# Eight smallest experts on 64 slots, with unsplit float32 weights on column parts of TensorE, placed among the dense tiles

## The chip, the cores and the metric

The kernel runs on one core of one Trainium2 chip. The metric is the device time of one execution in microseconds (us). One profiled execution of the kernel before is read besides; its time is given beside its span.

## What is computed

Two blocks follow each other on 256 tokens of width 1024, in float32: a first block (attention, a linear recurrence, a mixture of experts) and a second block of two layers. The change touches the mixture of experts alone. Cut to that, the reference is:

```python
def hierarchical_moe(h, w_group, b_group, w_er, b_er, w_gate, w_up, w_down):
    # one group of 4 experts for a token, and the 2 best experts in it
    ...
    combine_w = jnp.sum(jax.nn.one_hot(expert_id, N_EXPERTS) * top_w[..., None], axis=1)
    def expert_block(args):
        xs, cs = args
        a = jnp.einsum('nd,edf->nef', xs, w_gate)     # 16 experts, 1024 -> 512
        u = jnp.einsum('nd,edf->nef', xs, w_up)
        hid = jax.nn.silu(a) * u * cs[:, :, None]
        return jnp.einsum('nef,efd->nd', hid, w_down) # 512 -> 1024
```

A token has a nonzero weight for two of the 16 experts only. Each expert has 6 MB of weights: gate, up and down.

## The kernel before, in words

**Tiles.** All large weights are read as tiles of 1 MB (512 x 512 float32, laid out as 128 partitions x 4 x 512). SyncE's queue issues their loads in one fixed order into four landing buffers (`weights_raw`, `RAW_SLOTS = 4`), tile i into buffer i % 4 (`load_tile`). The product of two float32 numbers is made of three products of shorter ones: ScalarE rounds each half of a landed tile to `fp32r` (`high`, into `weights_high`), VectorE subtracts it from the landed numbers (`low`, into `weights_low`), and TensorE multiplies high by high, low by high and high by low. A landing buffer is free again when VectorE has made the second low half (`lo_ready`). The split copies lie in rings of two, in the mixture of three (`weights_high_third`).

**The mixture.** `M0 = T_MOE` is its first tile, and it has 96 tiles. The router's counts sort the experts by the number of their tokens. Expert 0 is computed for all 256 tokens before the order is known. Of the sorted list, the three fullest are "dense" (`DENSE = 3`): all 256 tokens, 48 matmuls of 256 columns or 24 of 512 for each tile (`feature_tile`, `down_tile`, `token_rows`). The other twelve are "sparse" (`SPARSE = 12`): an expert gets 128 slots; matmuls with one-hot matrices gather its tokens (`gather_chunk`, two experts at a time, four chunks), and a tile is then 12 matmuls whose stationary operand is the slots and whose moving operand is 512 columns of weights (`item_tile`). The hidden numbers go through SiLU on ScalarE and a product on VectorE, are turned by four transposes (`turn_hidden`), split, and multiplied by the two down tiles (`item_down`). GpSimd scatters each expert's rows into an array in HBM (`pairs`), reads it back at the end (`pair_rows`), and VectorE adds the rows, two for each token (`add_pairs`).

**The order.** It is written out by hand on each engine. The twelve sparse experts come first, each one's down tiles after the next one's gate and up tiles; then the three dense experts follow. Near the end stand the up tiles of dense expert 3, the two down tiles of dense expert 2, and the two of expert 3. While TensorE works on expert 2's down tiles, the hidden numbers of expert 3 are made (`dense_hidden` on VectorE, `dense_high` on ScalarE, and the low part on VectorE). `add_pairs` is called before the last dense expert's tiles are split.

## Time and profile before

| | us |
|---|---|
| median of 3 runs | 1275.63 (1275.31 to 1275.70) |
| the profiled execution | 1276.64 |
| its span | 1274.8 |
| TensorE busy | 1212.1 (95%) |
| VectorE busy | 888.7 (70%) |
| ScalarE busy | 783.6 (61%) |
| weights split on VectorE in all (368 + 64 halves) | 443.8 + 77.0 |
| weights split on ScalarE in all | 383.1 + 67.9 |

The profiled execution's time is its span and 1.8 us around it. In the rows below, busy TensorE time is no measure of its peak: matmuls are pipelined, so that one record of 0.39 us starts 0.23 us after the last. The distance between starts is the cost of one, and the idle time in front of an instruction (in brackets) says what ended last there. The span's times are in us from its start. The sparse experts' gate and up tiles run from 347.6, the dense experts after them, and the last tile of the mixture leads to the first rows of the result at 673.4.

### The profile page before, as it was taken

What the parts mean: (1) busy time and instruction counts of PE and PEld (TensorE: products, weight loads), DVE (VectorE), ACT (ScalarE), POOL (GpSimd) and SP (SyncE); (2) the same over time, 40 slices, a digit from 0 to 9 for tenths busy, and PEclk for the clock granted to TensorE, in tenths of its full rate; (3) what the DMA queues carried; (4) which work ended last, traced back from release to release, by engine and by line L of the source; (5) the groups of instructions that cost most, each with busy time, mean ns of one, the idle gap of its engine ahead of it and who ended that gap; (6) DMA issues with size and microseconds to landing.
All of it is one profiled execution on the core that took longest, in us unless ns stands there. A gap on an engine that the chain in (4) does not pass through costs nothing.

```text
span 1274.8 us, 19255 instructions
## 1 busy us (share of the span) xinstructions
PE 1212.1 (95%) x7779; PEld 1081.4 (85%) x7779; DVE 888.7 (70%) x1204; ACT 783.6 (61%) x1226; POOL 32.1 (3%) x42
## 2 busy tenths in 40 slices
PE   7999898998999999999999999999999998999997
PEld 7987788998888888889997888899987887899995
DVE  5839986667999999885576646465586556455676
ACT  6568666645588888884345557556535557555543
POOL 1000000000000000000000000000010000000000
PEclk9999999999999999999999999999999999999999
DMA  9743543443589999997763454444345543445331
GB/s 364 254 164 99 165 133 100 145 161 124 199 293 321 328 349 344 335 365 279 247 197 127 142 177 132 133 133 159 106 137 183 162 166 105 160 132 166 100 133 50
DMA packets 117754, 241.22 MB, mean 189 GB/s; under 512 B 5202, under 2 KB 7282, under 8 KB 116769
## 3 DMA queue, kind: packets, MB, share of 16 engines
q1 hardware_dynamic: 113088, 228.44, 53.1%
q0 software_dynamic: 3376, 8.93, 1.9%
q10 hardware_dynamic: 1200, 2.61, 0.6%
q8 instruction: 62, 1.02, 0.3%
q14 instruction: 28, 0.22, 0.1%
HBM read 235.38 MB, written 9.44 MB: 192 GB/s over the span
## 4 chain that ended last, share of the span: by engine, by line
PE 77%; DVE 13%; ACT 6%; issue 3%; DMA 1%; SPq 0%; DVEq 0%; ACTq 0%
PE psum L562 26%; PE psum L1256 15%; PE psum L488 12%; DVE weights_low L364 4%; PE psum L501 4%; PE psum L2138 3%; PE psum L1246 3%; PE psum L2182 2%; PE psum L2198 2%; PE psum L1273 2%; PE psum L2172 1%; PE psum L2117 1%; PE psum L535 1%; ACT weights_high L355 1%; ACT arena L868 1%
## 5 line engine op out<-in xcount | busy, mean ns | idle before, releaser
L364 DVE TENSOR_TENSOR weights_low<-weights_raw,weights_high 128x1024 fp32r<-128x1024 f32 (+1 forms) x368 | 443.8, 1230 | 154.8 <-ACT weights_high L355 151.8
L355 ACT ACTIVATE weights_high<-weights_raw 128x1024 fp32r<-128x1024 f32 (+1 forms) x368 | 383.1, 1057 | 202.6 <-PE psum L562 88.3
L562 PE MATMUL psum<-act_high,weights_high 128*128 128x256 f32 x912 | 265.6, 291 | 2.2 <-ACT arena L2218 1.6
L562 PE MATMUL psum<-act_low,weights_high 128*128 128x256 f32 x912 | 258.5, 283 | 0.0
L562 PE MATMUL psum<-act_high,weights_low 128*128 128x256 f32 x912 | 258.5, 283 | 0.0
L562 PEld LDWEIGHTS psum<-act_high,weights_high 128*128 128x128 f32 x912 | 175.2, 192 | 6.2 <-issue 3.4
L562 PEld LDWEIGHTS psum<-act_high,weights_low 128*128 128x128 f32 x912 | 175.4, 192 | 0.5 <-issue 0.5
L562 PEld LDWEIGHTS psum<-act_low,weights_high 128*128 128x128 f32 x912 | 175.1, 192 | 0.0
L488 PE MATMUL psum<-weights_high,act_high 128*128 128x512 f32 (+1 forms) x320 | 127.7, 399 | 7.9 <-DVE weights_low L364 5.0
L488 PE MATMUL psum<-weights_high,act_low 128*128 128x512 f32 (+1 forms) x320 | 124.6, 389 | 0.0
L488 PE MATMUL psum<-weights_low,act_high 128*128 128x512 f32 (+1 forms) x320 | 124.5, 389 | 0.0
L355 ACT ACTIVATE weights_high_third<-weights_raw 128x1024 fp32r<-128x1024 f32 x64 | 67.9, 1063 | 50.2 <-PE psum L1256 23.5
L364 DVE TENSOR_TENSOR weights_low_third<-weights_raw,weights_high_third 128x1024 fp32r<-128x1024 f32 x64 | 77.0, 1222 | 22.1 <-ACT weights_high_third L355 21.2
L488 PEld LDWEIGHTS psum<-weights_high,act_high 128*128 128x128 f32 x320 | 60.1, 188 | 23.8 <-DVE weights_low L364 6.8
L488 PEld LDWEIGHTS psum<-weights_high,act_low 128*128 128x128 f32 x320 | 60.0, 188 | 12.7
L488 PEld LDWEIGHTS psum<-weights_low,act_high 128*128 128x128 f32 x320 | 60.2, 188 | 11.4
L1256 PE MATMUL psum<-weights_high,picked_high 128*128 128x512 f32 x144 | 57.1, 396 | 0.0
L1256 PE MATMUL psum<-weights_low,picked_high 128*128 128x512 f32 x144 | 56.8, 395 | 0.0
L1256 PE MATMUL psum<-weights_high,picked_low 128*128 128x512 f32 x144 | 56.8, 394 | 0.0
L2363 ACT ACTIVATE arena<-psum 128x512 f32<-128x512 f32 (+1 forms) x34 | 20.2, 595 | 55.7 <-PE psum L2172 55.7
L2353 ACT ACTIVATE arena<-arena,tiny 128x128 f32<-128x128 f32 (+2 forms) x80 | 33.0, 418 | 17.9 <-DVE tiny L2587 17.8
L2198 PE MATMUL psum<-mid_high,weights_high 128*128 128x256 f32 x128 | 36.5, 286 | 1.9 <-DVE mid_low L456 1.8
(448 smaller groups left out, 2361.3 us busy)
## 6 DMA issues: line engine op xcount, KB each, us to landing
weights_raw<-in_w_in SPq DMA_DIRECT2D x52, 1024.0 KB, 5.2
weights_raw<-in_w_expert_gate SPq DMA_DIRECT2D x32, 1024.0 KB, 6.6
weights_raw<-in_w_expert_up SPq DMA_DIRECT2D x32, 1024.0 KB, 6.5
weights_raw<-in_w_expert_down SPq DMA_DIRECT2D x32, 1024.0 KB, 5.7
weights_raw<-in_w_merge SPq DMA_DIRECT2D x32, 1024.0 KB, 5.0
weights_raw<-in_w_out SPq DMA_DIRECT2D x12, 1024.0 KB, 5.0
weights_raw<-in_w_branch SPq DMA_DIRECT2D x8, 1024.0 KB, 5.1
weights_raw<-in_w_lru_o SPq DMA_DIRECT2D x4, 1024.0 KB, 5.2
```

Source lines behind the costliest of these rows:

```text
L355: nc.scalar.activation(hi_tile(i)[:, half_at(part, n)], raw_tile(i, n)[:, cols], ACT.Copy)\
L364: dve.tensor_tensor(lo_tile(i)[:, half_at(part, n)], raw_tile(i, n)[:, cols], hi_tile(i)[:, half_at(part, n)].bitcast(f32), ALU.subtract). ...
L488: last = pe.matmul(pair(g)[:, t * 512:t * 512 + n], a[:, 4 * h + k, t * P:(t + 1) * P], b[:, chunk_at(k, n)], start=(h == 0 and k == 0 and ...
L501: return pe.matmul(pair(g)[:, t * 512:t * 512 + n], a[:, c0 + 4 * h + k, t * P:(t + 1) * P], b[:, chunk_at(k, n)], start=(h == 0 and k == ...
L562: last = pe.matmul(pair(g)[:, s * SEQ:(s + 1) * SEQ], b[:, k * 512 + s * P:k * 512 + (s + 1) * P], a[:, 4 * h + k, :], start=(h == 0 and k ...
L1246: last = pe.matmul(pair(g)[:, t * 512:(t + 1) * 512], a[:, c0 + k, t * P:(t + 1) * P], b[:, k * 512:(k + 1) * 512], start=(k == 0 and q == 0),
L1256: last = pe.matmul(out, a[:, k0 + k, cols], b[:, k * 512:(k + 1) * 512], start=(first and k == 0 and q == 0), stop=(final and k == 3 and q ...
L1273: last = pe.matmul(bank(5 + n % 2)[:, f * SEQ:(f + 1) * SEQ], part[:, t, fb * P:(fb + 1) * P], one_hots[q % 2][:, t, :], start=(t == 0 and ...
L2138: last = pe.matmul(at[:, h * SEQ:h * SEQ + n], qTs[0:rows_of(kind), h, t * P:(t + 1) * P], keys_of(kind, t, h), start=True, stop=True)
L2182: last = pe.matmul(bank(7)[:, HD * h:HD * h + HD], pTs[0:keys, (hh * kts + kt) * P:(hh * kts + kt + 1) * P], values_of(kind, kt, h), start ...
L2198: last = pe.matmul(pair(g)[:, s * SEQ:(s + 1) * SEQ], b[:, at:at + P], a[:, 2 * br + kc, :], start=(kc == 0 and q == 0 and s % 2 == 0), st ...
L2353: last = nc.scalar.activation(p[:, h, :], p[:, h, :], ACT.Exp, bias=l_nb[:, h:h + 1], accum_out=l_sum[:, h:h + 1])
```

## The change

Of the twelve sparse experts the first four stay as they are (`MEDIUM = 4`). The eight smallest get 64 slots each and are gathered four at a time. Their weight tiles aren't split: TensorE reads them from the landing buffer as plain float32, with the 64 slots as the stationary operand, in two halves that go to two column parts of the array (`tile_position` 0 and 64) and to the lower and the upper 64 partitions of the result. A landing buffer of such a tile is free when TensorE has used it. The dense tiles are now placed among them: behind each small expert's four gate and up tiles stand two dense tiles (even ones) or one (odd ones), then its own two down tiles. The gather of the small experts makes float32 rows (`picked_plain`) without a low part. `add_pairs` is the last but one thing that VectorE does. There are four landing buffers, as before.

```diff
-DENSE, SPARSE = 3, 12
+DENSE, SPARSE, MEDIUM = 3, 12, 4
...
+        SMALL_AT, at = [], T_MOE + 32
+        for j in range(SPARSE - MEDIUM):
+            SMALL_AT.append(at)
+            at += 6 + 2 - j % 2
+        AMID = [n for j, a in enumerate(SMALL_AT) for n in range(a + 4, a + 6 - j % 2)]
...
         def load_tile(sp, i, r=0, source=None):
-            if i >= RAW_SLOTS:
-                sp.wait_ge(lo_ready, halves_of(i - RAW_SLOTS + 1, r))
+            if i - RAW_SLOTS in PLAIN:
+                sp.wait_ge(tile_used, halves_of(i - RAW_SLOTS + 1))
+            elif i >= RAW_SLOTS:
+                sp.wait_ge(lo_ready, split_halves(i - RAW_SLOTS + 1, r))
...
+        def small_tile(pe, i, out, stationary, first, final):
+            pe.wait_ge(raw_ready[i % RAW_SLOTS], 16 * (i // RAW_SLOTS + 1))
+            for k in range(4):
+                for h in range(2):
+                    at = 512 * k + 256 * h
+                    last = pe.matmul(out[64 * h:64 * h + 64, :], stationary(k), raw_tile(i)[:, at:at + 256],
+                                     start=(first and k == 0), stop=(final and k == 3), tile_position=(0, 64 * h),
+                                     skip_group_check=True)
+            last.then_inc(tile_used, 2)
...
+            for k in range(4):
+                at = P * (k % 2) + 64 * (k // 2)
+                for n, tile in enumerate(tiles_n):
+                    last = pe.matmul(small_out_bank(i)[64 * n:64 * n + 64, :], hidT_n[:, at:at + 64],
+                                     raw_tile(tile)[:, 512 * k:512 * k + 512], start=(k == 0), stop=(k == 3),
+                                     tile_position=(0, 64 * n), skip_group_check=True)
...
             if c == 3:
-                for j in range(2):
-                    for t in range(NT):
-                        last = pe.matmul(bank(7)[:, 64 + 4 * q + 2 * j:66 + 4 * q + 2 * j],
-                                         one_hots[q % 2][:, t, j * P:(j + 1) * P], rows_r[:, t, DENSE + 2 * q + j, :],
-                                         start=(t == 0), stop=(t == 1))
+                for i in members(q):
+                    n = slots_of(i).stop - slots_of(i).start
+                    for at in range(0, P, n):
+                        for t in range(NT):
+                            last = pe.matmul(bank(7)[at:at + n, 64 + 2 * i:66 + 2 * i],
+                                             one_hots[q % 2][:, t, slots_of(i)].bitcast(f32),
+                                             rows_r[:, t, DENSE + i, :].bitcast(f32), start=(t == 0), stop=(t == 1),
+                                             tile_position=(0, at))
...
         def moe_pe(pe):
...
+            for i in range(MEDIUM, SPARSE):
+                beside, *more = AMID_TILES[i - MEDIUM]
+                small_gate_up(pe, i)
+                dense_tile(*beside, 0, 2)
+                turn_small(pe, i)
+                dense_tile(*beside, 2, 4)
+                for tile in more:
+                    dense_tile(*tile)
+                small_down(pe, i)
+            for h in range(2):
+                dense_tile(DENSE, "u", h)
             pe.wait_ge(hid_lo, DENSE + 2)
...
         def moe_act(act):
...
+            for i in range(MEDIUM, SPARSE):
+                beside, *more = AMID_TILES[i - MEDIUM]
+                high(act, DENSE_AT[beside])
+                small_silu(act, i)
+                for tile in more:
+                    high(act, DENSE_AT[tile])
+                if i == SPARSE - 1:
+                    high(act, M0 + 92)
+                small_turned(act, i)
...
+                small_out(act, i)
...
         def moe_dve(dve, own):
...
+            for n in range(93, 96):
+                low(dve, M0 + n)
+            dense_hidden(dve, DENSE)
+            dve.wait_ge(block_free[(DB_DOWN[DENSE - 1] + 1) % 2], (DB_DOWN[DENSE - 1] + 1) // 2 + 1)
+            add_pairs(dve, own)
```

TensorE's row before, in the sparse stage, where an expert's gate tile ends, the last expert's hidden numbers are turned and the next tile begins:

```order
L1256 MATMUL psum<-weights_high,picked_low 128x512
L1348 MATMUL psum<-params,arena 128x128 [waits sparse_hidden_low,sparse_hidden]
L1348 MATMUL psum<-params,arena 128x128 x3
L1256 MATMUL psum<-weights_high_third,picked_high 128x512 [waits lo_ready]
L1256 MATMUL psum<-weights_low_third,picked_high 128x512
```

TensorE's row now, from the last split tile of a sparse expert over the four unsplit gate and up tiles of the first small one to its first dense tile:

```order
L1289 MATMUL psum<-weights_high,mid_low 128x512
L1299 MATMUL psum<-weights_raw,arena 64x256 [waits raw_ready0,picked_high]
L1299 MATMUL psum<-weights_raw,arena 64x256 x7
L1299 MATMUL psum<-weights_raw,arena 64x256 [waits raw_ready1,picked_high]
L1299 MATMUL psum<-weights_raw,arena 64x256 x7
L1299 MATMUL psum<-weights_raw,arena 64x256 [waits raw_ready2]
L1299 MATMUL psum<-weights_raw,arena 64x256 x7
L1299 MATMUL psum<-weights_raw,arena 64x256 [waits raw_ready3]
L1299 MATMUL psum<-weights_raw,arena 64x256 x7
L577 MATMUL psum<-act_high,weights_high_third 128x256 [waits lo_ready,block_free1,sparse_out]
```

TensorE now waits for the landing itself (`raw_ready`) at each unsplit tile, and for a split one (`lo_ready`) right behind them.

ScalarE's row now, at the last small expert: its SiLU, the split of the first up tile of dense expert 3, and only then the copy of the turned hidden numbers (L1592):

```order
L1586 ACTIVATE arena<-psum 128x256 [waits sparse_hidden,tile_used]
L370 ACTIVATE weights_high_third<-weights_raw 128x1024 [waits tile_used,raw_ready0]
L370 ACTIVATE weights_high_third<-weights_raw 128x1024 [waits tile_used]
L1592 ACTIVATE arena<-psum 128x256 [waits tile_used,sparse_turned]
L1535 ACTIVATE arena<-psum 128x1024 [waits hidden_low,tile_used]
L1597 ACTIVATE arena<-psum 128x512 [waits scattered1,tile_used]
```

A tile that lands behind both down tiles of that expert is split ahead of the copy that its down product needs.

VectorE's row before, at the same additions (L1765) of the pairs of rows:

```order
L1560 TENSOR_TENSOR mid_low<-arena,mid_high 128x1024 [waits hidden_high]
L364 TENSOR_TENSOR weights_low<-weights_raw,weights_high 128x1024 [waits hi_ready] x2
L1765 SCALAR_TENSOR_TENSOR x_tokens<-pair_rows,arena,x_tokens 128x1024 [waits pair_rows_in,block_free0]
L1765 SCALAR_TENSOR_TENSOR x_tokens<-pair_rows,arena,x_tokens 128x1024
L1765 SCALAR_TENSOR_TENSOR x_tokens<-pair_rows,arena,x_tokens 128x1024 [waits dve_own]
L1765 SCALAR_TENSOR_TENSOR x_tokens<-pair_rows,arena,x_tokens 128x1024
L364 TENSOR_TENSOR weights_low_third<-weights_raw,weights_high_third 128x1024 [waits hi_ready,dve_own]
```

VectorE's row now, at the mixture's end:

```order
L1675 TENSOR_TENSOR arena<-psum,arena 128x1024 [waits block_free0,tile_used]
L1678 TENSOR_TENSOR mid_low<-arena,mid_high 128x1024 [waits hidden_high]
L1895 SCALAR_TENSOR_TENSOR x_tokens<-pair_rows,arena,x_tokens 128x1024 [waits pair_rows_in,block_free1]
L1895 SCALAR_TENSOR_TENSOR x_tokens<-pair_rows,arena,x_tokens 128x1024
L1895 SCALAR_TENSOR_TENSOR x_tokens<-pair_rows,arena,x_tokens 128x1024 [waits dve_own]
L1895 SCALAR_TENSOR_TENSOR x_tokens<-pair_rows,arena,x_tokens 128x1024
L1989 SCALAR_TENSOR_TENSOR x_tokens<-psum,arena,x_tokens 128x512 [waits first_rows_out,block_free1,dve_own]
```

The four additions have moved from the middle of the dense experts to right ahead of the mixture's last additions (L1989).

## Rows read from the trace of the kernel before

**Rows 1.** Busy time by stretch: start:end, length, engines, PEclk, DMA share, GB/s.

```profile
0.00:32.00 32.00, 22.91 (x169) 22.57 (x170) 18.05 (x37) 19.55 (x31) 4.53 (x11) 1.00 0.98 365
347.00:569.00 222.00, 221.42 (x1072) 184.11 (x1071) 203.88 (x244) 182.80 (x227) 9.73 (x10) 1.00 0.96 331
```

**Rows 2.** TensorE's timeline: start, length, instruction, count.

```profile
347.25 0.50 PE L1279 MATMUL psum<-mid_low,mid_high 128*128 128x2 f32 x4
347.61 0.48 PE L1256 MATMUL psum<-weights_high,picked_high 128*128 128x512 f32 x1
...
351.48 0.39 PE L1256 MATMUL psum<-weights_high,picked_high 128*128 128x512 f32 x1
...
354.28 0.28 PE L1273 MATMUL psum<-mid_low,xn_high 128*128 128x256 f32 x1
...
355.23 0.40 PE L1256 MATMUL psum<-weights_high_third,picked_high 128*128 128x512 f32 x1
...
622.10 0.29 PE L562 MATMUL psum<-act_high,weights_high_third 128*128 128x256 f32 x1
...
627.87 0.28 PE L562 MATMUL psum<-act_high,weights_high 128*128 128x256 f32 x1
```

**Rows 3.** TensorE's timeline at plain float32 matmuls of 256 columns.

```profile
81.58 2.32 PE L644 MATMUL psum<-arena 128*128 128x256 f32 x10
```

**Rows 4.** The page's loads (KB, us to landing); GB/s in 40 slices of 347 to 569.

```profile
weights_raw<-in_w_merge SPq DMA_DIRECT2D x32, 1024.0 KB, 5.0
```

```profile
GB/s 230 186 338 300 269 364 369 348 285 337 239 383 366 336 350 340 307 265 371 381 336 362 322 285 293 374 370 317 383 322 258 323 385 384 352 367 345 347 387 372
```

**Rows 5.** The page's costliest groups: the splits, busy, mean ns, idle before.

```profile
L364 DVE TENSOR_TENSOR weights_low<-weights_raw,weights_high 128x1024 fp32r<-128x1024 f32 (+1 forms) x368 | 443.8, 1230 | 154.8 <-ACT weights_high L355 151.8
L355 ACT ACTIVATE weights_high<-weights_raw 128x1024 fp32r<-128x1024 f32 (+1 forms) x368 | 383.1, 1057 | 202.6 <-PE psum L562 88.3
```

**Rows 6.** VectorE's timeline at the mixture's end.

```profile
641.80 4.99 DVE L1765 SCALAR_TENSOR_TENSOR x_tokens<-pair_rows,arena,x_tokens 128x1024 f32<-128x1024 f32 x4
...
661.36 1.23 DVE L1560 TENSOR_TENSOR mid_low<-arena,mid_high 128x1024 fp32r<-128x1024 f32 x1 [1.12 <-ACT mid_high L1452]
...
673.43 1.41 DVE L1851 SCALAR_TENSOR_TENSOR x_tokens<-psum,arena,x_tokens 128x512 f32<-128x512 f32 x2 [4.17 <-PE psum L501]
```

**Rows 7.** GpSimd's timeline at the last scatter, and the read's us to landing.

```profile
596.68 0.77 POOL L1926 DMA_DIRECT2D pair_rows<-pairs  x1 [6.81 <-DMA pairs<-arena,pair_places]
```

```profile
pair_rows<-pairs POOLq DMA_DIRECT2D x1, 2048.0 KB, 10.3
```

**Rows 8.** TensorE's waits, whole span: us in total, times, longest.

```profile
PE psum L439 <- DVE arena L395: 12.3, 2, 8.7
...
PE psum L488 <- DVE weights_low L364: 5.0, 7, 2.5
PE psum L2117 <- issue: 4.2, 2, 2.1
PE psum L2172 <- ACT arena L2350: 4.1, 2, 2.0
```

**Rows 9.** Stretches behind those waits, in columns as Rows 1.

```profile
142.00:146.00 4.00, 3.61 (x15) 2.69 (x16) 4.00 (x5) 0.90 (x2) 0.00 (x0) 1.00 0.00 1
302.00:304.00 2.00, 1.71 (x9) 1.33 (x8) 2.00 (x5) 2.00 (x7) 0.00 (x0) 0.50 0.01 2
786.00:789.00 3.00, 3.00 (x17) 3.00 (x16) 2.42 (x6) 2.55 (x4) 0.00 (x0) 0.53 0.31 51
854.00:858.00 4.00, 4.00 (x46) 4.00 (x44) 2.86 (x3) 1.27 (x2) 0.00 (x0) 0.57 0.21 36
1080.00:1084.00 4.00, 3.53 (x28) 3.33 (x28) 3.42 (x7) 3.53 (x6) 0.00 (x0) 1.00 0.32 79
1148.00:1151.00 3.00, 3.00 (x33) 3.00 (x31) 1.95 (x2) 0.88 (x2) 0.00 (x0) 0.50 0.02 5
```

More of the change, by code:

```diff
@@ L1372, in moe_pe @@
             up_tile_by_rows(pe, M0 + 3, B0 + 1)
-            down_tile(pe, D_DOWN[0], DB_DOWN[0], halves=True)
+            down_tile(pe, D_DOWN[0][0], DB_DOWN[0], halves=True)
             for c in range(2):
                 gather_chunk(pe, 0, c)
-            down_tile(pe, D_DOWN[0] + 1, DB_DOWN[0] + 1)
+            down_tile(pe, D_DOWN[0][1], DB_DOWN[0] + 1)
             for c in range(2, 4):
                 gather_chunk(pe, 0, c)
-            for i in range(SPARSE):
-                q, cols = i // 2, slice((i % 2) * P, (i % 2 + 1) * P)
-                more = i % 2 == 0 and q + 1 < PAIRS
+            for i in range(MEDIUM):
+                q, cols = group_of(i), slots_of(i)
+                after = (1, None, 2, 3)[i]
                 if i % 2 == 0:
@@ L1525, in moe_act @@
                     pick_high(act, 3)
-            for i in range(SPARSE):
-                q, more = i // 2, i % 2 == 0 and i // 2 + 1 < PAIRS
+            for i in range(MEDIUM):
+                after = (1, None, 2, 3)[i]
                 for n in range(6 if i else 4):
-                    feed_moe(act, high, gate_at(i) - M0 + n)
-                    if more and n < 4:
-                        pick_high(act, 4 * (q + 1) + n)
+                    high(act, gate_at(i) + n + 3)
+                    if after and n < 4:
+                        pick_high(act, 4 * after + n)
                     if n == 1 and i:
@@ L1814, in moe_dve @@
             pair_places(dve, own, 0)
-            for i in range(SPARSE):
-                q, more = i // 2, i % 2 == 0 and i // 2 + 1 < PAIRS
+            for i in range(MEDIUM):
+                after = (1, None, 2, 3)[i]
                 for n in range(6 if i else 4):
-                    feed_moe(dve, low, gate_at(i) - M0 + n)
-                    if more and n < 4:
-                        pick_low(dve, 4 * (q + 1) + n)
+                    low(dve, gate_at(i) + n + 3)
+                    if after and n < 4:
+                        if after < 2:
+                            pick_low(dve, 4 * after + n)
@@ new lines, in moe_dve @@
+                        if after:
+                            pair_places(dve, own, after)
+            low(dve, M0 + 31)
+            item_low(dve, MEDIUM - 1)
+            for i in range(MEDIUM, SPARSE):
+                beside, *more = AMID_TILES[i - MEDIUM]
+                low(dve, DENSE_AT[beside])
+                small_hidden(dve, i)
+                for tile in more:
+                    low(dve, DENSE_AT[tile])
+                if i == SPARSE - 1:
+                    low(dve, M0 + 92)
+                for d, part, h in (beside, *more):
+                    if (part, h) == ("u", 1):
+                        dense_hidden(dve, d)
+                    if part == "d":
+                        dense_add(dve, d, h, DB_DOWN[d] if h else DB_DOWN[d - 1] + 1)
@@ L1881, in moe_sp @@
             before = None
-            for i in range(SPARSE):
+            for i in range(MEDIUM):
                 e = expert(DENSE + i)
@@ L1888, in moe_sp @@
                 before = e
-            for d in range(1, DENSE + 1):
-                e = expert(d - 1)
-                gate_up(wg, D_GATE[d], e)
-                if d < DENSE:
-                    down(down_at(SPARSE - 1) if d == 1 else D_DOWN[d - 1], before)
-                gate_up(wu, D_UP[d], e)
-                if d == DENSE:
-                    down(D_DOWN[d - 1], before)
-                before = e
-            down(D_DOWN[DENSE], before)
+            wide = expert(0)
+            for h in range(2):
+                dense_load((1, "g", h), wide)
+            down(down_at(MEDIUM - 1), before)
+            for i in range(MEDIUM, SPARSE):
+                e = expert(DENSE + i)
+                gate_up(wg, gate_at(i), e)
+                gate_up(wu, up_at(i), e)
+                for tile in AMID_TILES[i - MEDIUM]:
+                    if tile[1:] == ("g", 0):
+                        wide = expert(tile[0] - 1)
+                    dense_load(tile, wide)
+                down(down_at(i), e)
+            for part in "ud":
+                for h in range(2):
+                    dense_load((DENSE, part, h), wide)
         def clear_pairs(pool):
```

264 lines of the change are left out of this document (160 added, 104 removed).

## The prediction

> **What bounds the kernel now.** I read the busy times by stretch first. In the sparse stage TensorE is busy for 221.4 of 222.0 us, at full clock, while the DMA engines carry 331 GB/s and are busy for 0.96 of the time [rows 1]. So two resources are near their ends at once: TensorE has no gap, and the loads could go only a little faster. The span's first 32 us, all loads, carried 365 GB/s [rows 1], and single slices of the sparse stage reached 387 [rows 4]. Second, the timeline gives the price of each kind of work by the distance between starts: a sparse tile takes 2.80 us (351.48 to 354.28), a gather chunk 0.95 (354.28 to 355.23), a dense tile 5.77 (622.10 to 627.87), four place matmuls 0.36 [rows 2]. Checked against the whole: from 347.61 [rows 2] to the mixture's first finished rows at 673.43 [rows 6] are 325.8 us; 72 sparse tiles (201.6), 20 chunks (19.0), 5 groups of place matmuls (1.8), 12 groups of four transposes at some 0.5 (6.0) 16 dense tiles at 5.75 (92.0) and two last half tiles (5.6) give 326.0. The stretch is bound by TensorE's own work, end to end.
>
> **The small experts' tiles.** A plain float32 matmul of 256 columns stands in the trace as two records; ten records take 2.32 us [rows 3], the last one's tail of some 0.38 in it (0.39 for a split tile's record [rows 2]), so the starts are 0.216 us apart. A small tile has 8 such matmuls, 16 records: 3.45 us one after the other, 1.73 if the two column parts work at once. No row of before shows two parts at once, so these are the ends. I take 1.75 to 1.8: the two parts have different columns of the array, different PSUM partitions and different results, and only the issue is shared, for which one record each 0.216 us leaves room.
>
> The Trainium skill says the same in "TensorEngine Tiling (Array Packing)", section "Key Properties": different tiles can load weights and multiply in parallel; no run here shows it. Against it stands "TensorE: Matmul & The Clock Gate", section "Part 3: Packing small matmuls", where a weight load overlaps with running matmuls only in another row group, and column parts share all rows. By that rule alone each of a tile's 16 loads would stand open. For the full array the trace disagrees: weight loads are busy for 184.1 us beside TensorE's 221.4 of 222.0 in the same row group [rows 1].
>
> **The loads become the bound.** A tile of 1.05 MB at 365 GB/s takes 2.87 us (2.71 at 387, 3.17 at 331) [rows 1, 4], and a load that is alone 5.0 us from issue to landing [rows 4]. I let a tile land 5.0 after its issue, but not before 2.87 after the last. There are four buffers, and an unsplit tile now keeps its buffer until TensorE has used it, where a split one gave it back ahead. Follow an even expert from the end of the last down tiles (0), its two gate tiles already landed:
> - the loads of the two up tiles start at 0: they land at 5.0 and 7.87. The gate tiles are used by 3.6;
> - the first dense tile's load takes the first gate tile's buffer at 1.8 but stands behind both: it lands at 10.74. Its first half is split 1.06 + 1.23 later [rows 5]: 13.03;
> - two dense tiles and the transposes: 13.03 + 11.5 + 0.5 = 25.0. The copy by ScalarE 0.4, the two down tiles, landed long ago, 3.5: **28.9 us**. TensorE has stood for 1.4, 1.1 and 3.4 us.
>
> An odd expert has one dense tile less: 23.2. The first one finds all four tiles landed: the dense tile lands at 6.8 and the up tiles end at 7.2, so it takes 25.0. Eight: 25.0 + 23.2 + 3 x 52.1 = **204.5 us**. The speed of the small tiles enters that only with the two down tiles.
>
> The same work before: 48 x 2.80 + 12 x 5.75 + 12 x 0.95 + 8 x 0.5 + 3 x 0.36 = 219.9. So 15.4 us are won there, not the 48 x 1.0 that TensorE's own work falls by.
>
> **What stands around them.** (a) The first four experts: 22 tiles 61.6, twelve chunks 11.4 (of the stretch's 20 before, eight fell on these experts; four move here from later, eight go away), transposes 1.5, and the place matmuls, now plain float32: 0.7 and, for the two groups of four experts, 32 short records each at the 0.09 of [rows 2], 2.9 twice: 81.0 in all. (b) Dense expert 1's gate tiles and the fourth expert's down: 11.5 + 0.5 + 5.6 = 17.6. (c) At the last small expert ScalarE splits an up tile of dense expert 3 before it copies the turned hidden numbers. That tile lands at 19.4 of that expert's cycle and its split ends at 21.5, where TensorE wants the copy at 18.9: +3.0. (d) Up tiles of dense expert 3: 11.5. (e) Its hidden chain was covered by expert 2's down tiles. Now nothing covers it: a product on VectorE, the 1.12 wait for ScalarE, the low part of 1.23 [rows 6], some 3.6. (f) The first rows, two half tiles: 5.6. (g) The pairs: ScalarE's copy behind the last down tile is some 0.7 (estimate, half of the 1.06 of a split half [rows 5] and a start), the issue 0.8, the scatter lands 6.8 later, the read takes 10.3 [rows 7] and the additions 5.0 [rows 6], so they end at 23.6, where TensorE's first rows are ready at 11.5 + 3.6 + 5.6 = 20.7. The rows of the result are queued behind them on VectorE, and the next layer's transposes wait for those: 2.9. Before, the additions ran at 641.80, 31 us ahead of need.
>
> Sum: 81.0 + 17.6 + 204.5 + 3.0 + 11.5 + 3.6 + 5.6 + 2.9 = 329.7, against 325.8: **+3.9 us**.
>
> **The clock.** Before, TensorE is never idle in this stretch. Behind the kernel's start its waits of 2.0 us or more are six: 3.6, 2.5, twice 2.1, twice 2.0 [rows 8] (the 8.7 is the start). Behind four of them the granted clock stands at 0.50 to 0.57 of full, the lower of the two levels, 1.2 GHz; behind the ones at 142 and 1080 at 1.00 [rows 9]. Each of the eight experts now has such a wait of up to 3.4 us, and right behind it the dense tile on which the end depends. The stretch of 4.0 us at a mean of 0.57 had 3.4 us at half [rows 9], which cost 1.7 of work at full clock; four of six times, eight times: **+9.1 us** (0 to 13.6). Emptying the array when it goes from whole to parts and back, some four times an expert, has no row: 0 to 0.2 each, and I take 0.
>
> The sum against the profiled execution is 1276.6 + 3.9 + 9.1 = 1289.6. That execution is 1.0 above the median of the runs, so the forecast is 1289.
>
> **Rivals.**
> - *The loads and the clock do better*: two or three loads in flight land at 2.71, the waits don't lower the clock, the two late steps (c) and (g) hide. From 1289: - 9.1 - 2.6 (16 steps of 0.16) - 3.0 - 2.9 = 1271. For it: slices at 387 GB/s; two of six waits without a fall. Against: scatters share the queues, and four buffers are held longer. Chance 0.27, 1262 to 1276.
> - *The column parts work one after the other*: 3.45 us a small tile, slower than the split tile's 2.80. Then an even expert takes 4 x 3.45 + 0.5 + 11.5 + 0.4 + 6.9 = 33.1 and an odd one 27.35, TensorE never waits, and the stage takes 241.8: 1275.6 + 3.9 - 3.0 + 37.3 = 1314. It decides from a small tile of 3.26 us on: four of them reach the 13.03 at which the dense tile is ready, and each further 0.1 us costs 4.8. For it: no row shows parts at once. Chance 0.18.
> - *The change doesn't do what it says*: the buffers are refilled in time and TensorE's saving shows: without waits a small expert is 10.6 of small tiles, 0.5 + 0.4 and its dense tiles, 161 us in all in place of 204.5, some 1236. Against: the chain above, in which a load can't be issued before the buffer is empty. Chance 0.02.
> - By the skill's rule on weight loads alone the small tiles would be far above 3.45, each load of 64 columns at up to the 0.19 of a record: an estimate over 1350. Chance 0.02.
>
> **How the numbers follow.** My case, the loads as bound with falls of the clock: 0.51, 1274 to 1302. Its lower edge, with few falls, reaches into no change. About 0.2%, 2.6 us, is what a measurement can tell from none. Faster: 0.24 of the first rival, 0.02 of the third, 0.02 of my case: 0.28. Same: 0.07 of my case and 0.03 of the first rival: 0.10. Slower: 0.42 of mine, 0.18 and 0.02: 0.62. The range takes in the serial case: 1265 to 1316.
>
> **What would show it.** In the changed kernel: the starts of a small tile's records, in pairs, 1.75 us a tile (right) or 3.45 (wrong). Waits of TensorE for the loads of `weights_raw` at L1299, and for the split behind them, some 6 us an expert, and a cycle of 52 us for two experts. The granted clock at half behind the long ones. A wait of some 3 us for ScalarE at the last small expert, of 3.6 at the hidden numbers of dense expert 3, and VectorE's additions of pairs ending after the first rows. The DMA engines at some 310 GB/s in the small stage. If TensorE has no waits there and the stage still takes 205, the reasons are wrong though the time is right.

## The result, and the profile after

| | before | changed |
|---|---|---|
| median of four runs each, us | 1275.61 (1275.31 to 1275.70) | 1295.85 (1292.86 to 1298.55) |
| ratio, 95% interval | | 1.0159 (1.0136 to 1.0181) |
| profiled execution / its span, us | 1276.6 / 1274.8 | 1298.55 / 1296.8 |
| stretch from the first sparse expert's first tile (347.61, now 348.62) to the mixture's first rows, us | 325.8 | 346.1 |

The changed kernel is slower by 1.6%; 1289 was forecast, within 1265 to 1316. Of the 22.0 us that the span grew by, 20.3 lie in the stretch that the prediction summed.

The view of busy time by stretch of the changed kernel (start:end, length, TensorE, its weight loads, VectorE, ScalarE, GpSimd, granted clock, DMA share, GB/s). The first row is the first four experts, the second the small experts' stage, the third the tail; the last is a stretch behind one of TensorE's waits:

```profile
347.61:443.70 96.09, 95.96 (x580) 82.59 (x578) 72.45 (x99) 67.61 (x90) 4.34 (x3) 1.00 0.80 276
443.70:673.00 229.30, 180.78 (x1162) 127.08 (x1162) 45.20 (x48) 42.49 (x57) 8.75 (x9) 0.90 0.75 272
673.00:698.00 25.00, 21.34 (x121) 18.57 (x119) 14.86 (x15) 8.32 (x11) 1.36 (x2) 0.93 0.96 375
569.00:573.00 4.00, 3.78 (x19) 3.81 (x20) 3.91 (x5) 2.04 (x3) 0.00 (x0) 0.57 1.05 387
```

Where [rows 1] had TensorE busy for 221.4 of 222.0 us beside 331 GB/s, it now stands for 48.5 us of the small experts' stage, and the loads run at only 272 GB/s. Neither resource is at its end. The loads' rate over forty slices of that stage shows how: it swings between some 390 and nothing, as the loads start together when TensorE gives the buffers back and then have no buffer to go to.

```profile
GB/s 123 384 388 230 0 238 399 387 282 133 367 390 387 212 12 350 381 387 174 84 370 393 387 250 0 300 398 368 236 197 397 388 375 130 12 269 399 387 234 78
```

TensorE's timeline at the first small expert: four small tiles, the first dense tile, and, 24.8 us in, the down matmuls (start, length, instruction, count, and in brackets the wait ahead):

```profile
443.70 7.13 PE L1299 MATMUL psum<-weights_raw,arena 128*64 128x256 f32 x64
453.91 0.55 PE L577 MATMUL psum<-act_high,weights_high_third 128*128 128x256 f32 x1 [3.08 <-DVE weights_low_third L379]
...
468.49 3.65 PE L1340 MATMUL psum<-weights_raw,arena 128*64 128x512 f32 x16
```

Their 64 records take 7.13 us with the last one's tail. Their starts come in pairs, 0.216 us from pair to pair; in the run with eight buffers (below), where nothing is waited for here, the first dense matmul starts 7.05 us behind the first of these records. That is 1.76 us a tile: the two column parts work at once. Against [rows 2]'s 2.80 of a split tile TensorE's own work did fall by 1.0 us a tile. It was turned into waits. TensorE's waits from 340 to 700 (us in total, times, longest), where in [rows 1] it stood still for 0.6 us of 222.0 in all, and those of the queue that issues the loads from 443.7 to 673:

```profile
PE psum L1299 <- DMA weights_raw<-in_w_expert_up: 23.1, 11, 4.2
PE psum L1279 <- DVE weights_low_third L379: 7.2, 2, 4.0
PE psum L577 <- DVE weights_low L379: 6.3, 2, 3.8
PE psum L1279 <- DVE weights_low L379: 6.0, 2, 3.2
PE psum L577 <- DVE weights_low_third L379: 5.4, 2, 3.1
PE psum L516 <- DVE mid_low L1678: 3.7, 1, 3.7
PE psum L1340 <- ACT arena L1592: 0.5, 1, 0.5
```

```profile
SPq L358 <- PE psum L1340: 89.8, 8, 13.3
SPq L358 <- PE psum L1299: 74.6, 32, 10.7
SPq L358 <- DVE weights_low L379: 23.3, 8, 4.3
SPq L358 <- DVE weights_low_third L379: 12.2, 4, 3.9
```

SyncE's queue waits for 164.4 us of these 229 until TensorE has used an unsplit tile. TensorE then waits 48.0 us for what those loads bring, directly (L1299) or through the split (L577, L1279). It is a loop: the loads start late and in bunches because the buffers are held, and the buffers are held because TensorE works late.

The queue's waits alone would not show that. In the kernel before, from 441.4 to 660, it waited 184.1 us of 219 for splits. There its longest wait was 7.1 us, here it is 13.3, and then several loads start together and stand behind one another: from issue to landing they take 7.8 to 9.3 us (medians by tensor), against 6.2 to 6.7 in the stretch of [rows 1].

One turn of it, by the queue's issues after a down pair that ended at 555.0, with each load's time to landing: the up tiles, issued at 555.2 and 555.7, land 5.9 and 8.3 later (561.1, 564.0), the first dense tile, issued at 557.0, 9.8 later (566.8). It is split at 569.0, and TensorE takes it at 569.2, 14.2 us into the cycle; 13.03 was forecast. These loads follow one another by 2.7 to 2.9, as forecast; the first one takes 5.9 and not the 5.0 of [rows 4]. Over the seven cycles behind the first it takes 5.5 to 7.6, with 5.9 in the middle, and most in the cycles that begin at 586.1 and 642.7 (6.6 and 7.6). In all seven GpSimd's scatter of the expert before was issued 1.6 us into the cycle, among these loads. No run took it away, so whether it slows them is not shown.

### The profile page after: what moved, and what is told of

It reads as the page before. It is cut to its first block and busy times, and to the rows that moved or that the text cites. A ratio compares the mean times of both kernels' runs of the same rounds, so it can differ in the third digit from the quotient of the medians.

```text
span 1296.8 us, 18998 instructions
## 1 busy us (share of the span) xinstructions
PE 1183.8 (91%) x7819; PEld 1027.8 (79%) x7819; DVE 754.7 (58%) x1063; ACT 671.4 (52%) x1106; POOL 33.6 (3%) x42
## 5 line engine op out<-in xcount | busy, mean ns | idle before, releaser
L379 DVE TENSOR_TENSOR weights_low<-weights_raw,weights_high 128x1024 fp32r<-128x1024 f32 x304 | 366.0, 1232 | 210.5 <-ACT weights_high L370 209.4
L370 ACT ACTIVATE weights_high<-weights_raw 128x1024 fp32r<-128x1024 f32 x304 | 314.1, 1055 | 227.1 <-PE psum L577 73.4
L577 PE MATMUL psum<-act_high,weights_high 128*128 128x256 f32 x928 | 272.4, 293 | 7.9 <-DVE weights_low L379 6.3
L577 PE MATMUL psum<-act_high,weights_low 128*128 128x256 f32 x928 | 264.8, 285 | 0.0
L577 PE MATMUL psum<-act_low,weights_high 128*128 128x256 f32 x928 | 264.6, 285 | 0.0
L577 PEld LDWEIGHTS psum<-act_high,weights_high 128*128 128x128 f32 x928 | 180.0, 194 | 12.5 <-DVE weights_low L379 7.2
L577 PEld LDWEIGHTS psum<-act_high,weights_low 128*128 128x128 f32 x928 | 180.3, 194 | 0.6 <-issue 0.5
L577 PEld LDWEIGHTS psum<-act_low,weights_high 128*128 128x128 f32 x928 | 180.0, 194 | 0.0
L379 DVE TENSOR_TENSOR weights_low_third<-weights_raw,weights_high_third 128x1024 fp32r<-128x1024 f32 x32 | 38.2, 1223 | 84.6 <-ACT weights_high_third L370 84.0
L1299 PE MATMUL psum<-weights_raw,arena 128*64 128x256 f32 x512 | 65.5, 412 | 23.1 <-DMA weights_raw<-in_w_expert_up 23.1
L1299 PEld LDWEIGHTS psum<-weights_raw,arena 128*64 128x64 f32 x512 | 38.2, 147 | 52.1 <-DMA weights_raw<-in_w_expert_up 29.9
L370 ACT ACTIVATE weights_high_third<-weights_raw 128x1024 fp32r<-128x1024 f32 x32 | 33.2, 1059 | 63.9 <-DMA weights_raw<-in_w_expert_up 23.7
L2506 ACT ACTIVATE arena<-arena,tiny 128x128 f32<-128x128 f32 (+2 forms) x80 | 33.0, 417 | 17.9 <-DVE tiny L2740 17.8
L2351 PE MATMUL psum<-mid_high,weights_low 128*128 128x256 f32 x128 | 36.2, 283 | 0.0
```

The lines of the kernel that those rows point to most:

```text
L370: nc.scalar.activation(hi_tile(i)[:, half_at(part, n)], raw_tile(i, n)[:, cols], ACT.Copy)\
L379: dve.tensor_tensor(lo_tile(i)[:, half_at(part, n)], raw_tile(i, n)[:, cols], hi_tile(i)[:, half_at(part, n)].bitcast(f32), ALU.subtract). ...
L577: last = pe.matmul(pair(g)[:, s * SEQ:(s + 1) * SEQ], b[:, k * 512 + s * P:k * 512 + (s + 1) * P], a[:, 4 * h + k, :], start=(h == 0 and k ...
L1299: last = pe.matmul(out[64 * h:64 * h + 64, :], stationary(k), raw_tile(i)[:, at:at + 256], start=(first and k == 0), stop=(final and k == ...
L2351: last = pe.matmul(pair(g)[:, s * SEQ:(s + 1) * SEQ], b[:, at:at + P], a[:, 2 * br + kc, :], start=(kc == 0 and q == 0 and s % 2 == 0), st ...
L2506: last = nc.scalar.activation(p[:, h, :], p[:, h, :], ACT.Exp, bias=l_nb[:, h:h + 1], accum_out=l_sum[:, h:h + 1])
```

## The experiments

All times are medians; the kernel before gave 1276.5, 1275.9 and 1276.6 us beside the three groups of runs. Two theories stood against each other at the start. **Mine**: the tiles' multiplication is cheap, and the turn of the four buffers sets the stage, with a price for the clock on top. **The rivals**: the clock is most of it; or the parts of the array are the price; or the tail is.

### Keep TensorE busy in its waits

```diff
+            for k in range(n):
+                pe.matmul(small_out_bank(i)[:, 0:256], act_hi[:, k % NC, 0:P], act_hi[:, k % NC, :], start=True,
+                          stop=True, skip_group_check=True)
```

(n is 16 and 6 ahead of the two up tiles and 20 ahead of the first dense tile.)

> The changed kernel with idle matmuls in TensorE's waits: per small expert 16 of them (128 x 256, 0.12 us each, 1.9 us) ahead of the first up tile, 6 ahead of the second, 20 (2.4 us) ahead of the dense tile, into a PSUM bank that is free then. They add nothing to the result and only take up waits for loads. Theory: the small experts' stage (226.2 us) is paced by landings, and the clock's falls cost only what lies behind the dense tile's start, some 8 us. So the clock goes back to full, the waits for loads_raw shrink by the filled time, the dense tiles start as late as before, and the time falls by about 8, to 1288. Rival: the clock is the main loss (44 us at half in that stage, 22 us of work): then 1274 to 1278. If the clock has no part: 1296.

1292.3 us (1289.5 to 1294.2), ratio 1.0114 (1.0086 to 1.0141). The stage's stretch and TensorE's waits in it:

```profile
443.00:668.00 225.00, 209.34 (x1504) 155.13 (x1504) 45.94 (x48) 42.54 (x57) 8.73 (x9) 0.99 0.77 278
```

```profile
PE psum L1299 <- DMA weights_raw<-in_w_expert_up: 6.5, 10, 1.5
PE psum L1352 <- ACT arena L1605: 3.3, 1, 3.3
```

The granted clock is 0.99 in place of 0.90: 3.4 us of the stage at half in place of 44.4. The stage falls from 226.2 to 221.1. The time falls by 5.7 by the two ratios to before (1.0159 and 1.0114, whose intervals just overlap) and by 3.6 by the medians. So holding the clock up does not bring the 20 us back; the rival of 1274 to 1278 falls. What it does cost has to be read in two parts, since the experiment added work. The time from the first dense matmul to the end of each cycle, summed over the eight, falls from 112.6 to 104.1. In that of the changed kernel is a wait of 0.5 at L1340 for ScalarE (the prediction's step (c)), in this one the same wait has grown to 3.3 (L1352 here); without them it is 112.1 against 100.8, so up to 11.3 us were the clock's. But the dense tiles start later by 3.4 in all, behind the added matmuls, and step (c) takes back 2.8. The net is 5.1.

### All of one part, then all of the other

```diff
-            for k in range(4):
-                for h in range(2):
+            for h in range(2):
+                for k in range(4):
```

(and the same turn in the down matmuls.)

> The changed kernel with one loop turned round: all matmuls of the lower column part of a tile, then all of the upper, so that neighbours never lie in different parts. Theory (two parts at once is what gives 1.76 us a tile): records 0.216 us apart, 3.45 us a tile, TensorE's waits for loads nearly gone, an even expert 33.1 and an odd one 27.4, the stage 242 in place of 226: 1311. Rival (parts are no faster, the spacing of records misleads): nothing changes, 1296.

1307.0 us (1305.3 to 1307.5), ratio 1.0235 (1.0214 to 1.0257). TensorE's timeline at the first four small tiles:

```profile
443.59 8.38 PE L1299 MATMUL psum<-weights_raw,arena 128*64 128x256 f32 x64
```

8.38 us, not the 13.8 of four serial tiles: the order in the program does not make the parts serial. The first four records of the 64 start singly, some 0.216 apart, the next 56 in pairs, the last four singly again, as if one part ran four records ahead of the other. The trace does not say which part a record belongs to, so that is a reading. The waits for loads stayed (17.4 us at L1299), where the expectation had them gone. So the number came near 1311 by a mechanism that did not hold, and the edit priced only a partly serial order. The next two runs do it properly.

### Both halves on one part, with four and with eight buffers

```diff
-                    last = pe.matmul(out[64 * h:64 * h + 64, :], stationary(k), raw_tile(i)[:, at:at + 256],
-                                     start=(first and k == 0), stop=(final and k == 3), tile_position=(0, 64 * h),
+                    last = pe.matmul(out[0:64, :], stationary(k), raw_tile(i)[:, at:at + 256],
+                                     start=(first and k == 0), stop=(final and k == 3), tile_position=(0, 0),
```

(and the same in the down matmuls. Both halves now write the same 64 rows of the bank as well, and the upper half's result is lost; the part and the rows change together in this edit.)

> The small tiles' and small down matmuls' two halves both go to the array's lower column part and to the same 64 rows of the bank (the upper half's result is left out), four landing buffers as in the changed kernel. So the two parts cannot work at once. Theory: a record of 64 columns takes 0.216 us alone, so a small tile takes 16 x 0.216 = 3.45 us in place of 1.76 and a down pair 16 x 0.43 = 6.9 in place of 3.65; TensorE's work grows by 32 x 1.7 + 8 x 3.3 = 81 us, of which up to the 66 us by which the stage waits (226.2 against 159.4 with eight buffers) could hide some, but the buffers are held longer too: 1320 to 1346. The serial rival of the prediction said 1314. Rival, that column parts give no speed of their own and TensorE's waits hide the rest: 1296 to 1305.

> The same with eight landing buffers (the upper halves' results are left out here too): TensorE is then never waiting for loads, and the whole price of serial parts shows: 1231.3 + 81 = 1312, small tiles 3.45 us each, down pairs 6.9. Rival, that the array pipelines records of one part as it does those of two: 1231 to 1245.

1316.7 us (1314.5 to 1319.9) with four buffers, ratio 1.0313 (1.0288 to 1.0339), and 1312.1 (1308.9 to 1313.5) with eight, ratio 1.0279 (1.0254 to 1.0304). TensorE's timeline at the first four small tiles, with four:

```profile
444.81 14.03 PE L1299 MATMUL psum<-weights_raw,arena 128*64 128x256 f32 x64
```

Its waits from 443 to 700, with four buffers:

```profile
PE psum L1340 <- ACT arena L1592: 2.9, 1, 2.9
PE psum L1279 <- DVE weights_low_third L379: 1.7, 1, 1.7
PE psum L1279 <- DVE weights_low L379: 1.4, 1, 1.4
PE psum L577 <- DVE weights_low L379: 0.9, 2, 0.6
```

Here a small tile is 3.5 us, and four buffers are enough: TensorE waits for 4 us of loads and splits, and the stage takes 246.7. With eight it takes 239.7, against the 159.4 of the run with eight buffers and both parts (below): the parts are worth 80.3 us where TensorE is the bound (81 were expected). With four they are worth 246.7 - 226.2 = 20.5. The other 60 are lost again in the buffers' turn, and in the clock that falls with its waits (44.4 us at half there, 3.4 here). My expectation for four, 1320 to 1346, was too high: it let the longer hold of a buffer delay the loads, where each load landed inside the longer work.

### More landing buffers

```diff
+        EXTRA = [9, 10, 5, 6]
+        def raw_slot(i):
+            if T_MOE + 32 <= i < T_MOE + 92:
+                return (i - T_MOE - 32) % (RAW_SLOTS + len(EXTRA))
+            return i % RAW_SLOTS
```

(EXTRA are slots of the arena that nothing uses in this stage; loads, splits and matmuls wait by the slot so found. With six buffers EXTRA is [9, 10].)

> The changed kernel with eight landing buffers for the 60 tiles of the small experts' stage (the four, and four parts of the scratch memory that are free by then: the two gathered halves of the second pair and the two token halves). Theory (a buffer held until TensorE has used it lets the loads stop and start, landings pace the stage): loads run on, no wait for a free buffer, 60 tiles at 2.8 to 2.9 us are 172, TensorE's own work is 161, so the stage takes 175 to 185 in place of 226 and the time is 1246 to 1256. Rival 1 (the DMA engines or the clock set the pace, not the buffers): at most 5 us, 1291. Rival 2 (one expert's chain from up tile over SiLU and hidden numbers to the down tiles is the bound): some 10 us, 1286.

> Six landing buffers in the small experts' stage in place of four (eight gave 1231.3, four 1295.9). Theory of the buffer's turn: with four buffers the stage's 60 tiles took 226.2 us, 3.77 us a tile, so a buffer turned in 4 x 3.77 = 15.1 us (landing, then held until TensorE is done). If the turn stays the same, six buffers give 15.1 / 6 = 2.5 us a tile, just under the 2.66 (159.4 / 60) that TensorE itself took with eight: then nearly all of the gain is there, 1231 to 1242. Rival, that the gain comes with the buffers in proportion because more loads in flight make each land later (a turn that grows): half of it, about 1264.

Eight: **1231.3 us** (1228.7 to 1236.2), ratio 0.9654 (0.9626 to 0.9683), faster than both kernels. Six: 1247.8 (1244.6 to 1249.7), ratio 0.9784 (0.9763 to 0.9805). The stage's stretch with eight, its loads' rate in forty slices of 443.3 to 602, and what is left of TensorE's waits from 443 to 670:

```profile
443.00:602.00 159.00, 155.19 (x1135) 110.82 (x1136) 44.28 (x46) 39.90 (x54) 7.78 (x8) 1.00 1.00 379
```

```profile
GB/s 409 399 395 387 394 233 291 373 400 388 399 405 409 407 391 389 407 409 403 395 388 403 404 409 403 388 392 406 410 407 392 392 407 405 409 398 378 215 391 58
```

```profile
PE psum L536 <- DVE mid_low L1698: 3.7, 1, 3.7
PE psum L536 <- DVEq L662: 2.6, 1, 2.6
PE psum L1360 <- ACT arena L1612: 1.8, 1, 1.8
PE psum L1299 <- DVE weights_low_third L399: 1.1, 1, 1.1
PE psum L597 <- DVE weights_low_third L399: 1.0, 1, 1.0
```

Nothing else in the program was touched, and 66.8 of the stage's 226.2 us are gone, with nearly all waits for loads and splits (2.1 are left) and every fall of the clock. The saving of TensorE's own work, which the change made and could not show, shows. It is more than expected (1246 to 1256): the 60 tiles took 2.66 us each, where I had 2.8 to 2.9. The loads ran at 379 GB/s over the stage, where 2.87 us a tile is 365 and the loads of the stage's first eight tiles had been issued before it began (four in the changed kernel). A load now takes 11 to 14 us to land (medians by tensor), behind others, and TensorE hardly waits for it. TensorE and the DMA engines are both near their ends here. The kernel before was not run with eight buffers; it had 0.6 us of idle TensorE in 222.0 [rows 1], so there was little there for more buffers to give.

With six the stage takes 177.6: 73% of the gain of eight. A buffer's turn is 15.1 us with four (4 x 226.2 / 60 tiles) and 17.8 with six. So neither of the two expectations holds as it stands: the turn grows with the number of buffers, but by less than it does. With eight, TensorE itself sets it.

### Half of each small tile's bytes

```diff
+            def loaded(source, tile):
+                return (source[:, 0:2, :], 256) if tile in PLAIN else (source, 512)
```

> Four landing buffers as in the changed kernel, but each of the small experts' unsplit tiles loads only the first two of its four blocks of rows, 0.5 MB in place of 1.05 (the other two hold what was there before, so the experts' results are not the reference's); TensorE, the dense tiles and all waits are the same. Theory, that the loads' bytes set when a dense tile can start: a load alone takes 5.0 us, of which 2.9 are transfer, so two half loads land at about 3.6 and 5.1 (5.9 and 8.7 measured with whole ones), the whole dense tile behind them at 8.0 and is split at 10.3 to 10.5, in place of the 14 to 15.7 measured. Seven cycles by 4 us and the first by 1: 29 us less, and up to 5 more where the clock no longer falls: 1262 to 1268. Rival, that a load's fixed time and the turn of the buffers set it and not its bytes: 1288 to 1296.

1278.0 us (1271.4 to 1282.8), ratio 1.0013 (0.9995 to 1.0031). TensorE's waits from 443.7 to 673, and the view of the loads from 443.7 to 600 on their time to landing:

```profile
PE psum L577 <- DVE weights_low L379: 8.6, 2, 5.0
PE psum L1279 <- DVE weights_low_third L379: 7.5, 2, 4.5
PE psum L577 <- DVE weights_low_third L379: 6.6, 2, 3.4
PE psum L1279 <- DVE weights_low L379: 6.1, 2, 3.1
PE psum L1299 <- DMA weights_raw<-in_w_expert_up: 5.1, 7, 1.4
```

```profile
weights_raw<-in_w_expert_gate SPq DMA_DIRECT2D x12, 512.0 KB, 3.8
weights_raw<-in_w_expert_up SPq DMA_DIRECT2D x12, 512.0 KB, 4.6
```

The bytes matter: the eight dense tiles start 21.5 us earlier in all (92.1 us into their cycles, not 113.6), and the time falls by 17.9. But 29 were expected from the dense tiles. A half load of a gate or up tile still takes 3.8 to 4.6 us to land, and the dense tile behind it still has its fixed part and its split: TensorE waits for the splits (L577, L1279) for 28.8 us, where the changed kernel had 24.9. So with four buffers that are held until they are used, the price is not the bytes alone: the fixed part and the split remain in it. Four more buffers, which hide all three, gained 3.6 times as much (64.6 us).

### Without the additions of the pairs

```diff
-            add_pairs(dve, own)
```

> The changed kernel without VectorE's four additions of the pairs of rows (the sparse experts' share is left out of the result) and without the wait for the rows ahead of the first result rows; the scatters and the read stay, their wait stands behind the mixture. Theory: in the changed kernel they end at 694.7 of its trace, where TensorE had the first rows at 691.2, so 3.5 us fall away: 1292. Rival (the next layer waits for something else then): no change, 1296.

1295.6 us (1292.3 to 1296.3), ratio 1.0136 (1.0111 to 1.0161). The first rows come 1.9 us sooner behind the last small expert (23.0 in place of 24.9), and TensorE's next wait, for the second half of the tokens, is 1.2 shorter (the changed kernel first, then without the additions):

```profile
PE psum L516 <- DVEq L642: 2.6, 1, 2.6
```

```profile
PE psum L516 <- DVEq L642: 1.4, 1, 1.4
```

That makes 3.1 us in the trace, near the 2.9 of step (g); the ratios to before (1.0159 and 1.0136) differ by 2.9 us too, but their intervals overlap and the medians differ by 0.3, so the time itself does not show it.

### The two late steps, with eight buffers

```diff
+                small_turned(act, i)
                 if i == SPARSE - 1:
                     high(act, M0 + 92)
-                small_turned(act, i)
```

```diff
-            add_pairs(dve, own)
+            add_pairs(dve, own, 0)
...
                 if t:
+                    add_pairs(dve, own, 1)
```

(the second with the pairs' rows read in two transfers.) The first run has both edits, the second the first edit alone.

> Eight landing buffers, and two waits of the tail taken away: ScalarE turns the last small expert's hidden part before it rounds the tile after it (a wait of 1.8 us in the run with eight buffers), and the pairs' rows come in two transfers, with the two additions of the second half of the tokens after the first half's normalization (without any additions the tail was 1.9 us shorter). Expected 1227 to 1230, 1.5 to 4 us under 1231.3; rival, that what these waits hid is next in line: 1231.

> Eight landing buffers and only the first of the two edits of the tuned version: ScalarE turns the last small expert's hidden part before it rounds the tile after it. It takes away a wait of 1.8 us: 1229.5 against 1231.3, the whole of what the tuned version gained; the halved additions then gave nothing net (TensorE's wait for the second half of the tokens grew from 2.6 to 4.1 us there). Rival: the additions gave the 1.6 and the queue nothing: 1231.3.

Both: 1229.7 us (1228.6 to 1230.1), ratio 0.9636 (0.9620 to 0.9653). The queue's edit alone: **1227.4** (1226.8 to 1228.0), ratio 0.9614 (0.9600 to 0.9627), the fastest of all. One of TensorE's waits from 600 to 680, with both:

```profile
PE psum L537 <- DVEq L663: 4.1, 1, 4.1
```

The wait for ScalarE is gone in both, and the stage is 2.0 us shorter (157.4 and 157.3 against 159.4), as step (c) says. Splitting the additions made the first rows come 1.4 us sooner than without (23.0 against 24.4 behind the last small expert), and then TensorE waited 4.1 us for the second half of the tokens where it had waited 2.6. It moved 1.5 us from one wait to the next, and the median is 2.2 us worse; what made it worse, and not only the same, stays open. The rival that the additions gave the gain falls. The queue's edit alone did better than expected (1229.5). Of its 3.9 us against eight buffers alone, 2.0 are seen in the stage; the rest is within that run's spread (1228.7 to 1236.2).

## Why the prediction was right, point by point

| stretch | forecast, us | measured, us |
|---|---|---|
| first four experts, dense 1's gate tiles, fourth down, (a) and (b) | 98.6 | 95.1 |
| eight small experts to their first dense matmul | 100.3 | 113.6 |
| from there to the end of each | 104.2, + 3.0 for (c), + 9.1 for the clock | 112.6 |
| tail, (d) to (g) | 23.6 | 24.9 |
| sum | 338.8 | 346.2 |

- **Small tiles**: right. 1.75 to 1.8 was taken, 1.76 measured. "Emptying the array" between whole and parts, put at 0 of 0 to 0.2, shows as little: with eight buffers the first dense record starts 0.31 us behind the last small one, 0.1 more than the usual distance. The serial rival had 3.45 and 1314; the run with both halves on one part had 3.5 and 1316.7. The rival fell only because the parts do work at once. Here the section "Key Properties" of "TensorEngine Tiling (Array Packing)" in the Trainium skill agrees: different tiles load their weights and multiply in parallel. The rule of "TensorE: Matmul & The Clock Gate", "Part 3: Packing small matmuls", that a weight load overlaps only with work in another row group, speaks against 1.76 us a tile and does not hold for these column parts.
- **Loads as the bound**: right as a mechanism and shown, by six and eight buffers and by half loads. With work of 3.5 us a tile on one part the same four buffers made TensorE wait for 4.0 us of loads and splits in all, nearly as the serial rival had it (none).
- **The step that was mis-sized** is "I let a tile land 5.0 after its issue": 100.3 forecast up to the first dense matmuls, 113.6 measured, +13.3. Seven cycles behind the first lost 12.2 of it: 7.9 in the first load (5.5 to 7.6 where 5.0 was put), 1.6 in the steps between landings (2.87 was put; 2.7 to 3.3, with one of 3.4 and one of 4.0), 1.5 in the issues, 0.2 us into the cycle each, and 1.2 in the splits. The first cycle lost 1.1, mostly because its dense tile landed 7.7 us in and not 6.8. The 5.0 came from loads of another weight (`in_w_merge`, read after 744 us), which land in 4.9 to 5.3. The same page of the kernel before had the experts' own loads:

```profile
weights_raw<-in_w_expert_gate SPq DMA_DIRECT2D x32, 1024.0 KB, 6.6
weights_raw<-in_w_expert_up SPq DMA_DIRECT2D x32, 1024.0 KB, 6.5
weights_raw<-in_w_expert_down SPq DMA_DIRECT2D x32, 1024.0 KB, 5.7
```

  The "310 GB/s in the stage" was 272 for the same reason. TensorE stood for 6.0 us an expert, as forecast, but partly by luck: the landings were later, and the small tiles, of which some ran at half clock (15.5 us at half ahead of the dense tiles), filled part of the time.
- **The clock**: 9.1 was forecast. The cycles' later parts had up to 11.3 of slower work, and the stage won 5.1 when the clock was held up. The difference is 3.4, by which the added matmuls made the dense tiles late, and 2.8, which step (c) took. So the term lay between 5 and 11; a clock held up for free was not tried. The stretch 569 to 573 at 0.57 is the pattern of [rows 9]. Of 15 waits of 2 us or more in the stage 11 had such a fall within 1.4 us of their end, and 44.4 us of the stage were at the lower level, 1.2 GHz.
- **(c)**, 3.0 forecast, though the prediction's own times give 2.2 to 2.6 (the split ends at 21.5, where its cycle of 23.2 less 3.5 and 0.4 has the copy begin at 19.3, and the text says 18.9): 0.5 in the changed kernel, since TensorE was late itself. As soon as it was not, the wait was there: 3.3 with the clock held up, 2.9 with both halves on one part, 1.8 with eight buffers. One edit takes it away.
- **(a)**: 98.6 against 95.1. The two groups of 32 place matmuls took 1.12 us each, 0.035 a record, not the 2.9 made of 0.09 a record, and that is the 3.5.
- **(e)**: 3.6 forecast, 3.7 measured, between TensorE's last up tile and the first rows. It is in every run, since no run put work there.
- **(g)**: 23.6 behind the last small expert for the end of the additions and 2.9 for their price. The timeline of VectorE has them as drawn:

```profile
689.73 5.00 DVE L1895 SCALAR_TENSOR_TENSOR x_tokens<-pair_rows,arena,x_tokens 128x1024 f32<-128x1024 f32 x4 [4.45 <-DMA pair_rows<-pairs]
694.76 1.41 DVE L1989 SCALAR_TENSOR_TENSOR x_tokens<-psum,arena,x_tokens 128x512 f32<-128x512 f32 x2
```

  They end 24.9 behind it, ahead of the first rows; the read took 11.5 us where 10.3 was put. Left out, they free 3.1 in two places of the trace; the time cannot tell, for its uncertainty is as large as the price itself.
- **The rivals**: "the loads and the clock do better" went wrong at the landings, which were later and not sooner. "The saving shows in full" needed twice the buffers: 1236 was worked out for it, and 1231.3 came with eight.

The stretch came out 7 us low from errors that partly offset, so the near hit owes something to luck: +13.3 for the landings, -3.7 for the clock and (c) together, -3.5 in (a), +1.3 in the tail. In the profiled execution another 1.7 of the span's 22.0 lie outside the stretch, and that execution is itself 2.7 above the median.

## What to carry to other kernels

A tile that is used as it landed holds its landing buffer until TensorE is done with it, where a converted one gives it back ahead. So an edit that removes the conversion and makes the matmuls shorter must be paid in buffers: count the longest chain from the release of a buffer to its next use (first landing, transfers behind one another, split), and give as many buffers as cover it. The same edit cost 20 us with four and gave 49 with eight and one reordered instruction. Take a load's time from loads of the stage in question, under its traffic (6.2 to 6.7 us here), not from the best row of the page (5.0).

## What the runs showed of the hardware

- Two column parts of 64 give the full factor of two on plain float32 tiles: 7.13 us for 64 records, 14.03 with both halves on one part. Order matters less than expected: grouped by part, the same 64 took 8.38.
- The loads reached 379 GB/s over 159 us, with slices at 400 to 410, above the 387 of the best slice in [rows 4], with eight buffers to go to; with six it was 348 over 177.6 us.
- A very short matmul can be cheaper than [rows 2] suggest: 32 records with two columns of data and 64 columns of the array, on two parts, took 1.12 us, where four on the whole array took 0.50.
- TensorE's clock fell behind 11 of 15 waits of 2 to 4.2 us in the small stage. Of the 44.4 us at half, 28.9 lay behind the start of a dense tile, where slower work is not hidden by a wait for loads. With the clock held up by added matmuls 5.1 us of the stage came back net, and up to 11.3 before what those matmuls cost elsewhere.
